# Projection that ends without waiting for its stores, and the sample rows' value pages in four column strips

## What is computed

```python
def _diff_attend(q1, q2, k1, k2, v, q_pos, k_pos, lam):
    ...
    w = probs(q1, k1) - lam * probs(q2, k2)
    return jnp.einsum('bhqk,bkhe->bqhe', w, v.astype(jnp.float32))

def _layer(x, p, conv_prev, h_prev, k_past, v_past, lw, lam_init):
    h = _rmsnorm(x, lw['norm_pre_mix'])
    u = h @ lw['w_in']
    xl, gl, q, k, v = jnp.split(u, SPLITS, axis=-1)
    ...
    o = _attend(q1, q2, k_all[..., :ATT_HD], k_all[..., ATT_HD:], v_all, q_pos, k_pos, lam)
    o = _rmsnorm(o, lw['subln_g'], eps=1e-5) * (1.0 - lam_init)
    ...
    mix = jnp.concatenate([lru_out, att_out], axis=-1) @ lw['w_out']
    x = x + _rmsnorm(mix, lw['norm_post_mix'])
    ...
    f = (jax.nn.silu(h @ lw['ffn_w_gate']) * (h @ lw['ffn_w_up'])) @ lw['ffn_w_down']
```

## Time and profile before

| | |
|---|---|
| median of 3 runs | 3083.38 us |
| the profiled execution, own time | 3086.3 us |
| its span | 3084.5 us, 38192 instructions |
| PE busy | 2924.5 us (95%), mean granted clock 0.98 |
| DVE, ACT, POOL busy | 58%, 44%, 8% |
| DMA | 402.57 MB, mean 131 GB/s |

### The profile page before, as it was taken

How to read it: one execution, slowest core, us unless ns; L and a number is a source line. 1 busy time by engine, 2 the same in 40 slices (tenths; PEclk the granted TensorE clock), 3 DMA queues, 4 the chain that set the end, 5 groups by cost and what they waited for, 6 DMA issues and landing times.

```text
span 3084.5 us, 38192 instructions
## 1 busy us (share of the span) xinstructions
PE 2924.5 (95%) x14240; PEld 2373.8 (77%) x14240; DVE 1799.1 (58%) x2873; ACT 1358.7 (44%) x2491; POOL 231.4 (8%) x314
## 2 busy tenths in 40 slices
PE   7999999679999999999999999999999999999997
PEld 6778787557677877787888777878888777787865
DVE  6867767557246566665566566655656565334454
ACT  5655645434234445544444455444444453222233
POOL 0201111200001010001101000111011000000000
PEclk9999999779999999999999999999999999999998
DMA  5546444756554444543534335525332353232221
GB/s 180 181 140 225 135 140 134 212 182 204 164 140 116 120 116 135 176 117 110 140 107 115 113 115 177 151 84 145 96 110 72 111 168 108 89 93 89 79 77 54
DMA packets 377575, 402.57 MB, mean 131 GB/s; under 512 B 25641, under 2 KB 277845, under 8 KB 377392
## 3 DMA queue, kind: packets, MB, share of 16 engines
q1 hardware_dynamic: 360624, 341.32, 37.4%
q0 software_dynamic: 16768, 58.81, 5.3%
HBM read 341.19 MB, written 58.91 MB: 130 GB/s over the span
## 4 chain that ended last, share of the span: by engine, by line
PE 57%; DVE 13%; ACT 6%; issue 3%; POOL 1%; DMA 0%; ACTq 0%; SPq 0%; DVEq 0%; POOLq 0%
PE c_bank L2649 45%; PE b_S L2941 3%; PE b_O L2967 2%; DVE c_w L2328 2%; DVE b_m L2535 2%; ACT b_p L2255 1%; PE b_S L2658 1%; PE b_WT L2953 1%; PE b_O L2658 1%; ACT c_junk L2098 1%; DVE b_p L2528 1%; DVE c_rows L2339 1%; DVE c_rows L2346 1%; PE b_S L2921 1%; DVE b_wT L2553 1%
## 5 line engine op out<-in xcount | busy, mean ns | idle before, releaser
L2649 PE MATMUL c_bank<-c_hT,c_w 128*128 128x512 f32 (+1 forms) x4416 | 1024.9, 386 | 15.3 <-DVE c_hT L2366 15.3
L2649 PEld LDWEIGHTS c_bank<-c_hT,c_w 128*128 128x128 f32 x4416 | 795.5, 190 | 170.7 <-issue 18.1
L2649 PE MATMUL c_bank<-c_w,c_fT 128*128 128x512 f32 x2112 | 508.4, 393 | 0.0
L2328 DVE TENSOR_TENSOR c_w<-c_raw,c_w 128x1024 fp32r<-128x1024 f32 x334 | 405.4, 1221 | 168.3 <-ACT c_w L2077 166.9
L2077 ACT ACTIVATE c_w<-c_raw 128x1024 fp32r<-128x1024 f32 x334 | 351.8, 1057 | 263.6 <-PE c_bank L2649 223.4
L2649 PEld LDWEIGHTS c_bank<-c_w,c_fT 128*128 128x128 f32 x2112 | 390.6, 188 | 86.3 <-issue 3.4
L2255 ACT ACTIVATE b_p<-b_S,b_nm 128x512 f32<-128x512 f32 (+3 forms) x288 | 180.2, 631 | 593.2 <-DVE b_nm L2536 593.2
L916 PE MATMUL a_bank<-a_w,a_hT 128*128 128x512 f32 x1152 | 284.3, 401 | 0.0
L2649 PE MATMUL c_bank<-c_w,c_hT 128*128 128x512 f32 x1152 | 273.9, 394 | 7.7 <-DVE c_w L2328 4.0
L2649 PEld LDWEIGHTS c_bank<-c_w,c_hT 128*128 128x128 f32 x1152 | 217.2, 190 | 54.8 <-DVE c_w L2328 4.7
L916 PEld LDWEIGHTS a_bank<-a_w,a_hT 128*128 128x128 f32 x1152 | 213.4, 188 | 51.9 <-issue 3.8
(11 more groups left out here) (374 smaller groups left out, 3346.5 us busy)
## 6 DMA issues: line engine op xcount, KB each, us to landing
c_raw<-in_ffn_w_gate SPq DMA_DIRECT2D x88, 512.0 KB, 4.8
c_raw<-in_ffn_w_up SPq DMA_DIRECT2D x88, 512.0 KB, 4.1
c_raw<-in_ffn_w_down SPq DMA_DIRECT2D x88, 512.0 KB, 4.0
a_raw<-in_w_in SPq DMA_DIRECT2D x40, 1024.0 KB, 5.3
b_k<-split_kT SPq DMA_DIRECT2D x72, 256.0 KB, 4.9
b_v<-split_v SPq DMA_DIRECT2D x36, 512.0 KB, 3.6
c_raw<-in_w_out SPq DMA_DIRECT2D x32, 512.0 KB, 5.5
c_raw<-in_ple_w_gate SPq DMA_DIRECT2D x32, 512.0 KB, 4.1
```

Source lines behind the costliest of these rows:

```text
L2328: V.tensor_tensor(w[:, e[1] % SLOTS, 1], raw[:, n % RAW], w[:, e[1] % SLOTS, 0].bitcast(F32), ALU.subtract).then_inc(split_ready, 1)
L2649: ins = T.matmul(out, lhs(k, a), rhs(k, b), start=first and k == 0 and n == 0, stop=end and k == blocks - 1 and n == 2)
```

## The change

The stores' semaphores of `project` become the caller's, so that they outlive its block. `project` returns three things: the semaphore and count for the sample rows' queries, those for its small stores, and the list of the other eight. The final waits move to the end of GpSimd's program in `attend_first`. SP there waits for the first group's `lru_out` before it loads from `mixT`, and for the sample queries' store before it loads them; ScalarE waits for the small stores before it writes the first weight slot.

The value pages of a sample row are multiplied into four strips of 32 partitions, one per page. VectorE picks the own head over 128 partitions, TensorE adds the strips with a further product (`fold`), and the rest of the sample rows' tail comes one item later, as do the first possible places for attention steps.

```diff
@@ project @@
-            pool.wait_ge(small_out, 16 * (LC + 5))
-            for n in range(ROWS):
-                pool.wait_ge(rows_out[n], 16 * sum(STORED[n::ROWS]))
-            for n in range(STAGES):
-                pool.wait_ge(stage_out[n], 16 * 12 * GROUPS // STAGES)
-            pool.wait_ge(lru_out, 16 * LC * GROUPS)
...
+    q_row = USE[GROUPS - 1, Q, TILES]
+    return ((rows_out[q_row % ROWS], 16 * stores_of_slot(q_row)), (small_out, 16 * (LC + 5)),
+            [(rows_out[n], 16 * sum(STORED[n::ROWS])) for n in range(ROWS)] +
+            [(stage_out[n], 16 * 12 * GROUPS // STAGES) for n in range(STAGES)] +
+            [(lru_out, 16 * LC * GROUPS)])
@@ attend_first @@
+            sp.wait_ge(lru_out, 16 * LC)
             for n in range(3):
                 load_entry(n)
+            sp.wait_ge(*q_row_out)
             sp.dma_start(table[:], io["page_table"].rearrange("(o b) n -> o (b n)", o=1)).then_inc(table_in, 16)
...
+            for out, count in stores_out:
+                pool.wait_ge(out, count)
...
+                    if n == 2:
+                        act.wait_ge(*small_row_out)
@@ feed @@
-    PLACES = [n for n in PLACES if n > FINISH + 3]
+    PLACES = [n for n in PLACES if n > FINISH + 4]
...
-        head = sb("d_head", [RH, HEADS])
+        head = sb("d_head", [P, HEADS])
+        fold = sb("d_fold", [P, RH])
+        parts = sb("d_parts", [P, P])
...
-        mine = sb("d_mine", [RH, HEADS, P])
+        mine = sb("d_mine", [P, HEADS, P])
...
-                if n == FINISH + 3:
+                if n == FINISH + 4:
                     sp.wait_ge(res_ready, 1)
...
-                if n == FINISH + 1:
+                if n == FINISH + 2:
                     act.wait_ge(to_act, 2)
...
-            link(V.reduce_sum(head[:], ident[0:RH, 0:RH].rearrange("p (b h) -> p h b", h=HEADS), axis=AX))
+            V.reduce_sum(head[:], ident[:].rearrange("p (b h) -> p h b", h=HEADS), axis=AX)
+            link(V.reduce_sum(fold[:], ident[:].rearrange("p (j r) -> p r j", r=RH), axis=AX))
...
                 if n == FINISH:
                     dve.wait_ge(vs_done, NS)
-                    link(V.tensor_tensor(mine[:], OT[0:RH].rearrange("p (h e) -> p h e", h=HEADS),
-                                         head[:].rearrange("p (h o) -> p h o", o=1).broadcast_to([RH, HEADS, P]), ALU.mult))
-                    link(V.reduce_sum(os_[:], mine[:].rearrange("p h e -> p e h"), axis=AX))
-
-                    link(V.scalar_tensor_tensor(os_[:], v32[:], wo[:], os_[:], ALU.mult, ALU.add))
+                    link(V.tensor_tensor(mine[:], OT.rearrange("p (h e) -> p h e", h=HEADS),
+                                         head[:].rearrange("p (h o) -> p h o", o=1).broadcast_to([P, HEADS, P]), ALU.mult))
+                    V.reduce_sum(parts[:], mine[:].rearrange("p h e -> p e h"), axis=AX).then_inc(to_pe, 1)
+                if n == FINISH + 1:
+                    dve.wait_ge(from_pe, 3)
+                    link(V.scalar_tensor_tensor(os_[:], v32[:], wo[:], PT[0:RH, 0:P], ALU.mult, ALU.add))
...
-                            ins = T.matmul(OT[0:RH], wz[:, b, j], pages[:, (NS + b) % 3, j], start=b == 0 and j == 0, stop=b == NS - 1 and j == PAGES - 1)
+                            ins = T.matmul(OT[j * RH:j * RH + RH], wz[:, b, j], pages[:, (NS + b) % 3, j], start=b == 0, stop=b == NS - 1)
                         ins.then_inc(vs_done, 1)
-                if n == FINISH + 2:
+                if n == FINISH + 1:
                     pe.wait_ge(to_pe, 3)
+                    T.matmul(PT[0:RH, 0:P], fold[:], parts[:], start=True, stop=True).then_inc(from_pe, 1)
+                if n == FINISH + 3:
+                    pe.wait_ge(to_pe, 4)
                     T.transpose(PT[:, 0:RH], os_[:], ident[0:RH, 0:RH]).then_inc(from_pe, 1)
```

More of the change, by code:

```diff
@@ L79, in project @@
     ident, ident_r, mask, nlam, sub_gain = shared
-    kk, vv, qq, k_in, v_in, q_in, held, free = ahead
+    kk, vv, qq, k_in, v_in, q_in, held, free, outputs = ahead
+    rows_out, stage_out, lru_out, small_out = outputs
     at = [first for first, _ in free]
@@ L233, in project @@
         rows_ready = sem("a_rows_ready")
-        rows_out = [sem(f"a_rows_out{n}") for n in range(ROWS)]
         qk_turned = sem("a_qk_transposed")
@@ L237, in project @@
         stage_lo = sem("a_stage_lo")
-        stage_out = [sem(f"a_stage_out{n}") for n in range(STAGES)]
         states_turned = sem("a_states_transposed")
@@ L241, in project @@
         states_out = sem("a_state_rows_ready")
-        lru_out = sem("a_lru_out")
         small_in = sem("a_small_in")
         small_ready = sem("a_small_ready")
-        small_out = sem("a_small_out")
         s_chain = sem("a_s_act_chain")
@@ L1109, in attend_first @@
     pages, qb, table, table_in, pages_in, qb_in, free = cached
-    kk, vv, qq, k_in, v_in, q_in, stored = ahead
+    kk, vv, qq, k_in, v_in, q_in, stored, lru_out, q_row_out, small_row_out, stores_out = ahead
     at = [first for first, _ in free]
@@ L2624, in _ @@
                     V.tensor_scalar(os_[:], os_[:], ors[:], None, ALU.mult).then_inc(to_pe, 1)
-                if n == FINISH + 2:
-                    dve.wait_ge(from_pe, 3)
+                if n == FINISH + 3:
+                    dve.wait_ge(from_pe, 4)
                     V.tensor_scalar(res[:].rearrange("p h b -> p b h"), PT[:, 0:RH].rearrange("p (b h) -> p b h", h=HEADS), sub_gain[:], None, ALU.mult).then_inc(res_ready, 1)
@@ L2996, in build @@
             free = ((base, turns), (turns + 80 * 1024, 224 * 1024))
+            rows_out, stage_out = ([sems.enter_context(nc.semaphore(f"a_{name}_out{n}")) for n in range(count)] for name, count in (("rows", 4), ("stage", 3)))
+            lru_out, small_out = (sems.enter_context(nc.semaphore(f"a_{name}_out")) for name in ("lru", "small"))
             with nc.cleanup_on_exit():
-                project(nc, io, split, pool_turn, shared, (kk, vv, qq, k_in, v_in, q_in, turns, free))
+                q_row_out, small_row_out, stores_out = project(nc, io, split, pool_turn, shared,
+                                                (kk, vv, qq, k_in, v_in, q_in, turns, free, (rows_out, stage_out, lru_out, small_out)))
             w = nc.alloc_sbuf_tensor_at("c_w", [P, 4, 2, 1024], F32R, offset=base)
@@ L3014, in build @@
             with nc.cleanup_on_exit():
-                attend_first(nc, io, split, pool_turn, shared, early, cached, (kk, vv, qq, k_in, v_in, q_in, stored))
+                attend_first(nc, io, split, pool_turn, shared, early, cached, (kk, vv, qq, k_in, v_in, q_in, stored, lru_out, q_row_out, small_row_out, stores_out))
             feed(nc, io, split, sems, pool_turn, shared, early, cached, stored)
```

## The result

The change makes the kernel faster: 3058.02 us (3054.46 to 3061.47) against 3084.48 (3082.0 to 3086.22), ratio 0.9913, 95% interval 0.9898 to 0.9929. That is 26.5 us, where 11.5 were forecast (3071.9 us). Both profiled executions show nearly the same: their own times are 3086.3 and 3058.49 us, 27.8 apart.

| term | predicted, us | in the traces, us | from |
|---|---|---|---|
| seam, last store to next load | −4.3 | −0.7 | 571.21 − 562.95 = 8.26 before; 570.69 − 563.12 = 7.57 after |
| eight value pages | −7.6 | −20.4 | 3.55 each before; 0.99 or 1.00 after |
| fold | +0.35 | +0.34 | its piece of the chain |
| attention steps | 0 | −5.3 | TensorE's waits there, added up below |
| sum | −11.5 | −26.1 | 1.7 of the 27.8 are in no term |

A forecast was written before the change was run, and what follows sets the result against it. TensorE, busy 95% of the span, was taken as the bound: −4.3 (seam) − 7.6 (pages) + 0.35 (fold) = −11.5 us, so 3071.9 us against the median, within 3067 to 3076; the rivals' range went from 3059, less 1, to 3081.

The forecast's parts named there:

- all-together: Rival for the value pages: all four strips run together, 20.5 us less over eight pages, 3059 us; chance 0.16.
- no overlap: Rival for the value pages: strips don't overlap, a page stays 3.55 us, only the seam is gained, 3079.5; chance 0.24.
- Part 2: Sample rows' value pages in four strips: 2.60 us a page instead of 3.55, 7.6 us less over eight pages.
- staircase: Value pages: a strip's second pass runs beside the next strip's first, 5 steps instead of 8; chance 0.50.
- Matmuls start in program order: Value pages: with both passes of a product sharing a strip, this gives 5 steps, 2.27 us a page before load delays.
- Weights are loaded one ahead: Value pages: each of three new strips starts 0.11 us late, making a page 2.60 us instead of 2.27.
- The best end of 0.99: Value pages: four strips run together in two steps, 0.99 us a page, 20.5 us less over eight pages.
- Part 1: Seam between projection and first attention stage: removing the wait at the projection's end gains 4.3 us.
- a drain right behind a store costs 2.87 us: Seam: GpSimd's drain time from the store's start, taken from the second seam, giving a gain of 4.3 us.
- The other end named: Seam: if the drain holds until the stores have landed, the next stage starts at 569.6, a gain of 1.6 us.
- Part 3: Sample rows' longer tail: a fifth product folding the strips costs TensorE 0.35 us, with no stall.
- Part 4: Attention steps: 79 of 150 move one item later; stalls taken as unchanged, 0 with 3 us either way.

The follow-up runs named there:

- two strips in blocks: Changed kernel, but a page's first two products go to one strip and the next two to another; 3062.95 us, one execution.
- experiment 4: Three edits of the changed kernel's strip choice: two strips alternating, two strips with consecutive products paired, one strip a page; 3063.08, 3062.95 and 3082.61 us.
- experiment 5: Changed kernel with the projection's last three stores issued by SyncE on its hardware queue instead of GpSimd; 3053.86 us, ratio 0.9900.
- the places alone: Kernel before with one number changed: the places of the attention steps begin one item later, moving 79 steps; 3078.23 us, ratio 0.9979.
- experiment 2: Kernel before with only the attention steps' places one item later, 3078.23 us; changed kernel with those places put back, 3065.11 us.
- the seam alone: Kernel before with only the waits at the projection's end moved to later users; 3082.5 us, ratio 0.9993.
- by turns: Changed kernel, but a page's four products alternate between two strips; 3063.08 us, one execution.

## Why the prediction was wrong

The direction was right and the size was not: the gain was 26.5 us, more than twice the forecast. The prediction names two ranges, 3067 to 3076 and, from all-together to no overlap, 3058 to 3081; the measured 3058.02 lies outside the first and on the edge of the second. The time came to the case to which 0.16 had been given (all four strips together, 3059), though two terms beside the strips differ from that case, the seam by 3.6 us less gain and the steps by 5.3 more. That the sum comes so near is partly luck, since the two cancel in part.

- **Part 2, the pages, was mis-sized: −20.4 and not −7.6.** The forecast's staircase rests on two sentences. "Matmuls start in program order" was true of a trace in which all products went to one strip, and falls with two strips in blocks (1.85 us a page). "Weights are loaded one ahead" was read from the earlier trace rows, where a single strip is at work; it holds for each strip apart, as the loads in experiment 4 show. The best end of 0.99 was the right number. The Trainium skill ("TensorE: Matmul & The Clock Gate", Part 3) has one rule on each side. It says that a weight load overlaps a matmul in flight only when the row groups differ. The trace disagrees: eight loads with the same rows fall within the first 0.16 us of the page's matmuls. The same section of the Trainium skill also has a model of packed tiles, the time of one matmul and a few ns for each further tile. The trace agrees in kind: four strips cost 0.99 us, two passes and the turn, which is the estimate of the sum rule for one product alone. From one strip to four a page became 3.55 / 0.99 = 3.6 times as fast.
- **Part 1, the seam: −0.7 in the trace and not −4.3.** The step that failed is "a drain right behind a store costs 2.87 us". GpSimd's drain lasts until its own stores have landed. At the second seam that store lands 2.6 us after its issue, a row of the kernel before that the prediction did not use; at the first seam, among the projection's other transfers, it takes 5.5 to 6.9 us. The other end named (the drain holds until the stores land, 1.6 us) was the right mechanism; at equal landing the gain is 2.8 − 1.4 = 1.4 us, over the ten traces above. In the four cases whose landing is shown above (the second seam of both kernels, the first of the changed one, experiment 5) the drain ended 0.3 to 0.4 us after it. That the new waits of later users cost nothing was right: the stage took 76.6 us, as before at the same clock, and the second seam's gap is 3.57 us (643.68 to 647.25), as before.
- **Part 3, the fold, was right:** 0.34 us against 0.35, and no gap on TensorE in front of it or of the transpose.
- **Part 4, the attention steps: −5.3 us of waits, and −6.5 us of time for the places alone, where 0 ± 3 stood.** The step that failed is "they fall anew rather than grow", at a mean of 0.7 us each. They are not alike: of the 11.6 us for b_p, 6.9 were three waits over 2 us (steps 9, 25 and 80), which the move ended, and it made two new ones. The mean hid that. A change of more than 3 us in these stalls was one of the prediction's own signs of being wrong. The gain of 6.5 us is shown by the runs, its cause only in part: the named waits hold some 3.8 of it over ten traces (experiment 2), and what makes some first tiles wait and others not stays open.

## What to carry to other kernels

Products that fill only 32 columns can go to separate column strips: four of them cost the estimated time of one here, and with two strips the order of issue made no difference. Taking away a wait for stores at a block's end gains little where GpSimd issued them: here 1.4 us, since its drain waited for their landing anyway. Moving the last stores to SyncE's queue let the next stage begin 4.2 us earlier; the wait for them then stands at the end of the next block. When an edit shifts a schedule by one place, list its stalls one by one before calling the shift neutral: here the shift was worth 6.5 us.

## What the runs showed of the hardware

- With stores of its own in flight, GpSimd's drain held for 2.3 to 8.3 us, until 0.3 to 0.4 us after its own last store's landing, where the landing was read; behind the waits for all stores it took 0.7 us. SyncE's drain took 0.2 to 0.3 us with its stores just issued.
- Weight loads ran one ahead in each column strip: two at once with one strip, four with two, eight with four (0.14, 0.15 and 0.16 us). Two strips took 1.84 us a page by turns and 1.85 in blocks, so neither waited for the other's place in the program.
- The granted clock of the first attention stage differed between executions of the same code, 0.63 to 0.71 over the same 232 matmuls, with 2.6 us between their stretches: more than the seam edit is worth. These are means over two levels. In the changed kernel and in the seam alone the stage began at 0.50 (1.2 GHz), behind 13 to 14 us without a matmul; the changed kernel then had 1.00 (2.4 GHz) from 598 to 614 us, the other from 586 to 610.
